# Two fp32 products of constants ahead of five long stretches of one-pass products with 256 columns

## What is computed

```
first block, layers 0 and 1 (h: 256 tokens, hc: 256 context tokens)
  h, hc += 0.5 * gate * swiglu(prenorm(h or hc), ffn1_w_in, ffn1_w_out)     # 1024 -> 2 x 2816 -> 1024
  h, hc += gate * (mixer(prenorm(.) @ w_in) @ mix_w_out)                    # layer 0: Fourier and gated linear
                                                                           # attention; layer 1: convolution and
                                                                           # differential attention
  h (and hc, in layer 0 only) += 0.5 * gate * swiglu(prenorm(.), ffn2_w_in, ffn2_w_out)
  h = rmsnorm(h)
second block, on h alone
  h = layer_norm(alpha * h + retention(h));          h = layer_norm(alpha * h + swiglu_ffn(h))
  h = layer_norm(alpha * h + dilated_attention(h));  h = layer_norm(alpha * h + swiglu_ffn(h))
```

## Time and profile before

| | us |
|---|---|
| runs | 2658.69, 2664.71, 2665.00 |
| median | 2664.71 |
| the profiled execution | 2665.84 |
| its span, first to last instruction | 2664.0 |
| TensorE busy | 2604.4 (98% of the span), 17444 matrix records |
| VectorE busy | 1482.9 (56%) |
| ScalarE busy | 1042.3 (39%) |

### The profile page before, as it was taken

How to read it: one execution, slowest core, us unless ns; L and a number is a source line. 1 busy time by engine, 2 the same in 40 slices (tenths; PEclk the granted TensorE clock), 3 DMA queues, 4 the chain that set the end, 5 groups by cost and what they waited for, 6 DMA issues and landing times.

```text
span 2664.0 us, 40437 instructions
## 1 busy us (share of the span) xinstructions
PE 2604.4 (98%) x17444; PEld 2298.8 (86%) x17444; DVE 1482.9 (56%) x1985; ACT 1042.3 (39%) x1402; POOL 199.0 (7%) x192
## 2 busy tenths in 40 slices
PE   6999999999999999999999999999999999999998
PEld 4788888877888888888888899999999999988998
DVE  4666654746556546553355665565555554565554
ACT  3322223634222224222233544443753454555544
POOL 0000000211000000000011000010020020144001
PEclk9999999999999999999999999999999999999999
DMA  7544445114434445443253175565455566663462
GB/s 256 179 159 152 153 163 168 51 61 158 142 135 163 138 135 185 139 150 102 63 173 111 52 232 176 162 210 161 156 167 179 171 198 186 203 150 112 156 203 85
DMA packets 376080, 405.98 MB, mean 152 GB/s; under 512 B 7264, under 2 KB 352176, under 8 KB 375904
## 3 DMA queue, kind: packets, MB, share of 16 engines
q1 hardware_dynamic: 375904, 403.40, 47.3%
HBM read 402.25 MB, written 1.12 MB: 151 GB/s over the span
## 4 chain that ended last, share of the span: by engine, by line
PE 91%; DVE 4%; ACT 2%; issue 2%; POOL 1%; DMA 0%; SPq 0%; DVEq 0%; POOLq 0%; ACTq 0%
PE bank L98 90%; DVE w_lo L109 1%; PE bank L101 1%; ACT w_hi L105 1%; POOL acc L109 1%; DVE tmp L117 0%; ACT x_hi L105 0%; DVE df_sc L126 0%; DMA ident<-in_ident 0%; ACT df_e L106 0%; DVE hT L117 0%; ACT at_pT L105 0%; DVE hT L109 0%; ACT L105 0%; DVE acc L109 0%
## 5 line engine op out<-in xcount | busy, mean ns | idle before, releaser
L109 DVE TENSOR_TENSOR w_lo<-w_raw,w_hi 128x2048 fp32r<-128x2048 f32 (+2 forms) x331 | 698.1, 2113 | 756.0 <-ACT w_hi L105 755.4
L98 PE MATMUL bank<-x_hi,w_hi 128*128 128x256 f32 (+1 forms) x3000 | 981.8, 328 | 6.2 <-DVE x_lo L117 2.6
L98 PE MATMUL bank<-x_hi,w_lo 128*128 128x256 f32 (+1 forms) x3000 | 972.6, 325 | 0.0
L98 PE MATMUL bank<-x_lo,w_hi 128*128 128x256 f32 (+1 forms) x3000 | 968.2, 324 | 0.0
L105 ACT ACTIVATE w_hi<-w_raw 128x2048 fp32r<-128x2048 f32 (+2 forms) x331 | 578.2, 1751 | 379.2 <-PE bank L98 227.1
L98 PEld LDWEIGHTS bank<-x_hi,w_hi 128*128 128x128 f32 x3000 | 565.4, 188 | 67.7 <-issue 16.3
L98 PEld LDWEIGHTS bank<-x_hi,w_lo 128*128 128x128 f32 x3000 | 568.1, 189 | 47.9
L98 PEld LDWEIGHTS bank<-x_lo,w_hi 128*128 128x128 f32 x3000 | 562.6, 188 | 46.8 <-issue 0.7
L98 PE MATMUL bank<-hid_hi,w_hi 128*128 128x512 f32 (+1 forms) x1056 | 355.9, 337 | 0.0
L98 PE MATMUL bank<-hid_hi,w_lo 128*128 128x512 f32 (+1 forms) x1056 | 354.2, 335 | 0.0
L98 PE MATMUL bank<-hid_lo,w_hi 128*128 128x512 f32 (+1 forms) x1056 | 354.0, 335 | 0.0
(11 more groups left out here) (276 smaller groups left out, 2329.4 us busy)
## 6 DMA issues: line engine op xcount, KB each, us to landing
w_raw<-in_ffn_w_in SPq DMA_DIRECT2D x88, 1024.0 KB, 5.7
w_raw<-in_ada_w SPq DMA_DIRECT2D x72, 1024.0 KB, 7.9
w_raw<-in_ffn_w_up SPq DMA_DIRECT2D x44, 1024.0 KB, 5.2
w_raw<-in_attn_w_in SPq DMA_DIRECT2D x36, 1024.0 KB, 5.5
w_raw<-in_ffn_w_out SPq DMA_DIRECT2D x32, 768.0 KB, 4.7
w_raw<-in_ret_w_in SPq DMA_DIRECT2D x24, 1024.0 KB, 5.2
w_raw<-in_ffn_w_out SPq DMA_DIRECT2D x32, 640.0 KB, 4.3
w_raw<-in_odd_w_in SPq DMA_DIRECT2D x12, 1024.0 KB, 5.5
```

Source lines behind the costliest of these rows:

```text
L98: return Issued(self.eng and self.eng.matmul(out, lhsT, rhs, start=start, stop=stop, skip_group_check=loose))
L109: return Issued(self.eng and self.eng.tensor_tensor(out, a, b, op))
```

## The change

A new function `pe_realign` takes a bank in turn, takes it out of the books again as `pe_keep_busy` does, and issues two fp32 products: the identity matrix is stationary, the first 256 columns of the table of small constants (`small_t`) are moving. Nobody reads the result and no semaphore is raised. It is called in five places: in `pe_ffn` ahead of `j` = 4 where n is 256 (that is `b1`, `c0` and `c1`), at the head of `pe_deep_out`, and in `pe_dilated` behind the three products of `at_onehot`. Only TensorE's stream has new rows.

```diff
+def pe_realign(e):
+
+    k = e.k
+    bank = e.bank("spare", None, None)
+    del e.used[k.bank_at["spare"]]
+    for _ in range(2):
+        e.matmul(bank[:, 0:T], k.ident[:, :], k.small_t[:, 0:T], True, True)
...
             else:
+                if j == 4 and n == T:
+                    pe_realign(e)
                 for base in range(2):
...
 def pe_deep_out(e, s, w, x, n):
     k = e.k
+    pe_realign(e)
     for c in range(KC // 2):
...
                 e.matmul(bank[0:16, 0:384], rel[0:32, 16 * g:16 * g + 16], t.oh[:, g, :], True, True).then_inc(
                     k.product, ("bias_rows", g))
+            pe_realign(e)
             k.after(4, sp_bias_rows)
```

## The result

The changed kernel takes 2668.5 us in the median (2662.31 to 2674.62, 21 runs), the kernel before on the same chip 2654.67 us (2646.48 to 2665.0, 21 runs). The ratio is **1.0049**, 95% interval 1.0039 to 1.006: the change is slower by half a per cent, 13.0 us. The forecast was 2646.5 us, 2641 to 2662, faster. It missed the time, the range and the sign. One run of the kernel before (2855.41 us, beside experiments 12 to 14) had a granted clock of only 0.863 and is left out of the ratios. The profiled execution took 2671.23 us, its span is 2668.9.

The account below looks back on a forecast made before the run. TensorE, busy 98% of the span, was taken to bound the kernel. From the profiled 2665.84 us, less 22.6 given back plus 4.4 price made 2647.6, or 2646.5 us against the median of 2664.71; range 2641 to 2662.

Parts of the forecast that it names:

- The price: At all five places, each added pair costs 0.87 us of TensorE time, 4.4 us in all.
- A pair of full fp32 products of 256 columns as fast, in five cases out of five: Retention's pairs leave fast, so the added pairs should speed the stretches behind all five places, giving back 22.6 us.
- third rival: All five places: constants lie elsewhere in memory, long stretches stay slow, only the price is left; 2669.1 us, chance 0.15.
- All of them are slow before: Stretches behind the five places, 5136 products, all run at the slow 117.7 ns, so each gains 4.4 ns.
- one layer's stretch of 1439 at the fast pace would be 6.3: Feed-forward layer: a chance fast stretch is worth 6.3 us; the lowest run before lay 6.0 us under the median.
- Held to the stretch's end: Behind all five places the fast pace lasts to the end of each stretch, part of the 22.6 us.
- second rival: Feed-forward layers: fast pace lost at the first change from `x` to `hid`; 2659.8 us, chance 0.12 shared with partial failures.
- No new wait at the fast pace: In b1, weights wanted 4% sooner still arrive in time, so no new wait arises.
- slower rival: All five places: the pair deals a third pace, 120.0 ns per product; 2680.9 us, chance 0.04.
- The two other places: Retention's output (384 products) and attention's second part (576): less alike, forecast fast; rival without them 2650.7 us, chance 0.17.
- The rule against the change: All five places: a product's gap is 109 ns whatever ran before, so nothing is given back and only the price stays.

Follow-up runs that it names:

- experiments 12 to 14: Against the kernel before: one fp32 product in four places, 128 columns in attention, 2649.12 us; four products per place, 2652.53 us; the kernel before unchanged, 2658.22 us.
- experiment 8: The change with columns of `small_t` from 64 bytes in as stationary operand instead of the identity; 2652.94 us, ratio 1.0007 to the kernel before.
- experiment 4: Pairs or other numbers of fp32 products ahead of every `j` from 4 to 20 in b1, c0 and c1, against the kernel before; 2680.27 us.
- experiment 11: The change again, unedited, against the kernel before; 2668.65 us, ratio 1.006.
- experiment 5: The change with one fp32 product in place of two in each place; 2650.44 us, ratio 0.9954 to the kernel before.
- experiment 6: The change with pairs in b1, c0 and c1 alone, none in retention or attention; 2667.86 us, ratio 1.0019 to the kernel before.
- experiments 1 and 14: The kernel before, unchanged, for a second and a third profile; medians 2654.45 us (ratio 0.9999) and 2658.22 us.
- experiment 14: The kernel before, unchanged, for a third profile; 2658.22 us.
- experiment 9: Fillers ahead of each `j` step, four products alternating with pairs whose stationary operand starts at different bytes of `small_t`, against the kernel before; 2684.43 us.
- experiments 2 to 4: Against the kernel before: pair's moving operand 64 bytes on, 2669.15 us; 128 bytes on, 2666.45 us; fillers ahead of every `j` from 4 to 20, 2680.27 us.

## Why the prediction was wrong

*The price* was right: 4.4 us forecast for five, 0.98 us from the pair's start to the second product behind it in the earlier trace rows and in c0 after.

*"A pair of full fp32 products of 256 columns as fast, in five cases out of five"* is **the step that failed**, and with it the whole 22.6 us. The five cases were real, and in the sixteen traces here all 80 of retention's pairs of that kind (the second to the sixth of each trace) leave fast, but they have `rt_rot` as stationary operand and the change has the identity. The prediction took "128 x 128 stationary, 256 moving columns" for the same form. Experiment 8 shows that another stationary operand, its place and its values, is worth some 14 us, and experiment 4 that with the identity the outcome hangs on the pace before. The condition was written down, in the third rival ("the constants lie elsewhere in the on-chip memory"), with 0.15. Its time, 2669.1 us, lies 0.6 us from the measured median, but by a cancellation: its "no effect" was wrong too, as the pair turns the pace.

*The base* failed as well. "All of them are slow before" held for the profiled execution only. The three runs then known, 2658.69 to 2665.0, lay high: over 21 runs the median is 2654.67, ten under theirs. The kernel before has fast stretches by luck. In the thirteen traces up to experiment 11 (before and after among them), the stretch ahead of `j` = 4 was fast once in b1, six times in c0 and seven times in c1, 14 of 39. That is 14/39 x 4176 x 4.4 ns = 6.6 us, which the change loses. It also gives something back: at six of the 39 places of the thirteen traces with a filler the stall had left slow 2, from which the pair leaves fast (experiment 8's two places at 120 ns not counted), 6/39 x 4176 x 4.4 ns = 2.8 us. With the price of 4.4 the sum is **8.2 us**, against 13.0 measured by the ratio (10.4 to 15.9): the sign and the larger part of the loss, not all. The times suggest where the rest is, as an estimate. The two profiles of before with all three layers slow took 2665.84 and 2666.49 us, so the median of 2654.67 stands for some 11 us of fast stretches, 1.7 layers of three where the traces have 1.1; with 1.7 x 1392 x 4.4 ns = 10.4 us lost the sum is 12.0. The change's median lies 2.7 us under its all-slow profile, as the 2.8 asks. That executions without a profile are dealt more fast stretches than the profiled ones is not shown. Had every stretch been slow, a loss of 4.4 us, 0.17%, could hardly have been told. The prediction named the new deal in each run ("one layer's stretch of 1439 at the fast pace would be 6.3") and put it to the range's lower end only, not to the base.

*Held to the stretch's end* was right: experiment 5 is fast through `hid_hi` in b1, c0 and c1, so the second rival's mechanism was not seen. *No new wait at the fast pace* was right too, by the same run. *The slower rival's* third pace of the earlier trace rows came nowhere; the slower outcome had another cause, a stretch fast by luck turned slow by the pair, and that had no rival of its own.

*The two other places*: called less alike, they were just as slow under the change. Retention's output was slow behind the identity's pair in seven traces of seven and fast behind one and behind four products. In attention the pair was seen to change nothing: with nothing added the second part is slow behind a fast first part (before, experiment 6) and fast behind a slow one (experiments 1 and 14), and with the pair it is the same, six cases and one. One and four products left it slow behind a slow first part, one of 128 columns fast behind a fast one, two cases in two. So these turn what would otherwise have come, and no filler is shown to make this place fast from either pace.

*The rule against the change*: the Trainium skill's page "TensorE: Matmul & The Clock Gate", section "Back-to-back issue gap", gives the isolated gap of a product, an estimate of 109 ns for 256 columns. None of these stretches has it: they run at 113.3 and at 117.8 ns with the clock at 1.00, as in the trace before. What the prediction drew from it, that a filler changes nothing behind it, experiment 4 refutes.

What stays open: what the two paces and the two forms of slow are in the hardware, what it is in a stationary operand that decides, and what lets retention's pairs leave fast. Of the size of the loss some 5 us are not accounted for by the traces. The difference between experiment 6 and the change is 8.0 us by the ratios (1.0049 less 1.0019) and 0.6 by the medians, where the two places' price is 1.7. And I can't say why all three profiles of before lie above its median.

## What to carry to other kernels

Before a gain is summed over a stretch's pace, look at several profiles and some twenty runs of the kernel as it is: a pace that is dealt by chance has a mean, and the one profile at hand may be its worst case. A filler is only taken for like another if number, width and the stationary operand are the same, and its effect has to be asked for from each pace that can precede it. If a run of one-pass products is long, one fp32 product (2650.44 us against 2660.97, the one version that was clearly faster than before, though beside the slowest runs of before) or four (2652.53 against 2656.31, steadier but not told from no change) is worth trying where two aren't.

## What the runs showed of the hardware

- With one-pass products of 256 columns at clock 1.00, TensorE has a pace of 113.3 and one of 117.8 ns, each kept over more than a thousand products (experiment 14: 1414 records against 1361 in 160 us).
- An fp32 product of 256 columns with the identity as stationary operand moves between three conditions: two such products turn fast into slow 25 times in 26, and slow 2 into fast 11 times in 11. One product of 128 columns did the same (slow from fast 3 of 3, fast from slow 2 4 of 4).
- Which stationary operand the filler has decides as well (from fast, 64, 96, 160 and 192 bytes into `small_t` left fast, 0, 16, 32 and 128 slow; one case each in experiment 9). Place and values are not told apart. The start of its moving operand made no difference at 0 to 128 bytes (experiments 2 to 4); at 192 bytes stands the one exception.
- In attention the three fp32 products of 384 columns turned the pace round, fast into slow and slow into fast, in two traces each without a filler.
- Runs of one unchanged kernel on one core spread from 2646 to 2665 us. Some of that is this deal: one feed-forward layer on the other pace is 6.3 us.
